# A two-layer hybrid diffusion step on one core: projections in pieces between the steps of the scans, PSUM divided six banks to two

## The chip, the core and the metric

One core of a Trainium2 chip runs the whole program. Its engines run on their own and meet at semaphores: TensorE (PE, matmuls, with PEld for its weight loads), VectorE (DVE), ScalarE (ACT), GpSimd (POOL) and SyncE (SP, which issues most DMAs). Each takes its instructions strictly in the order of the program. SBUF holds the data; PSUM, in which matmuls leave their results, has eight banks of 512 fp32 columns. The metric is the time of the device in microseconds (us); lower is better.

## The reference, cut to what matters

Two layers, each over 128 context tokens and 512 latent tokens (640 in all, five tiles of 128), width 1024, all fp32:

```python
def layer(x, p, l, mod, ctx):
    x = half_ffn(x, 0, 0)                    # x + 0.5*gate * rmsnorm(swiglu(modulate(rmsnorm(x))))
    h = modulate(rmsnorm(x, g[2]), mod[:, 3], mod[:, 4])
    y, new = token_mixing(h, p, l, ctx)
    x = x + mod[:, 5][:, None] * rmsnorm(y, g[3])
    return half_ffn(x, 1, 2), new

def token_mixing(h, p, l, ctx):
    u = h @ p['w_in'][l]                     # 15 blocks of 256 columns, and 48 columns of gates
    ...  # A gated linear attention, C mLSTM, D retention: scans forward and backward over chunks, summed
    ...  # B attention: context to context; latent to a window of 16 columns with a bias, and to the cache
    y = concatenate([out_a, out_b, out_c, out_d]) @ p['w_out'][l]
```

## The kernel before

**Layout and precision.** Activations lie with features on the partitions: `xT` is the residual (8 blocks of 128 features by 640 tokens), `h2` the normed input as a high and a low part. Each large product is made of three matmuls (`three_pass`, L460 to L462: high by high, high by low, low by high). The weights are split into the two parts on POOL (`split`, L419 and L421: a copy that rounds to the high part, then a subtraction over the same 2048 columns for the low part), into two buffers `w_split` by turns. SP loads the raw weights in units of up to 1 MB into two slots (L363), each when the unit two before has been split or used.

**Units.** The layer is a list of 132 units. `U_FFN[0]` are the first FFN's (22 up units of 96 matmuls by 320 columns, 16 down units of 66; between the up units lie small units of the modulation, L471). Then come one unit of gates (160 columns), 15 of the input projection (four each for C, A and D, three for B) and four of the output projection (`U_OUT`), and then the second FFN. Unit n uses banks 0 to 3 or 4 to 7 (`half(n)`); PE takes it up when its split is done and the bank half was evacuated (`claim`: `split_done`, `unit_evac`). A unit of the projection is either `features` (result with features on the partitions, 2 x 2 x 8 x 3 = 96 matmuls of 320 columns) or `tokens` (5 x 8 x 3 = 120 matmuls of 256 columns). DVE, in a few cases ACT, evacuates a whole unit with one instruction of 1280 columns.

**The mixing.** PE's order is written out by hand: gates, five units (C's four and A's first), a wait until DVE and ACT have made the gate rows of C, turned copies of these rows (L613), then C's scans forward and backward, one unit, A with one unit ahead of each direction, two units, D, three units of B, the attention of B, the four output units. In a scan (`scan_group`, L622 to L661) PE first multiplies keys and values for the five tiles (L622), which DVE masks; DVE then carries the states along (L1341). After that a step per tile: scores of tile t+1 (L639; for C also L634), DVE's mask or decay (L1296, for C after an exponential on ACT), output of tile t (L654, L661), DVE's copy (L1304 to L1315). Scans use banks 0 to 7, so no unit of the projection runs inside one. After a group's two directions DVE norms the output per head (`head_norm`, L1369 to L1385, with a root from ACT, `head_rstd`), PE turns it (`concat`), ACT copies it to `catP`.

The attention of B runs 20 blocks (five tiles by four heads; the first four have 128 keys, the other 16 have 640): PE turns the probabilities of block b (L613), makes the scores of block b+2 (L460 to L462), multiplies by the values (L824); DVE adds the bias and finds the maximum (L1620 to L1628), ACT takes the exponential, DVE norms (L1637). The bias table is masked once before, at L1607. Then the four units of the output projection run, and the norm of their sum (`norm(3, ...)`, `add_square`, L1160, `sums`, L492) ends the stage.

## Time and profile before

| | us |
|---|---|
| median of 3 runs | 3450.99 |
| lowest, highest | 3434.47, 3455.9 |
| the profiled execution | 3443.74 |
| its span, first to last instruction | 3442.0 |
| PE busy in it | 3089.8 |
| PEld, DVE, POOL, ACT busy | 2914.7, 1176.2, 1143.6, 526.2 |

The page gives for each engine the time in which it had an instruction in work; a PE that is shown busy need not be at its full rate, since matmuls overlap and since its clock is granted at one of two levels (1.0 in the tables is 2.4 GHz, 0.5 is 1.2 GHz; the figure of a stretch is a mean). The two layers run the same program one after the other, so what is read in the first counts twice. In the first layer the mixing lies between 631.0 and 1198.8 us of the span.

### The profile page before, as it was taken

What the parts mean: (1) busy time and instruction counts of PE and PEld (TensorE: products, weight loads), DVE (VectorE), ACT (ScalarE), POOL (GpSimd) and SP (SyncE); (2) the same over time, 40 slices, a digit from 0 to 9 for tenths busy, and PEclk for the clock granted to TensorE, in tenths of its full rate; (3) what the DMA queues carried; (4) which work ended last, traced back from release to release, by engine and by line L of the source; (5) the groups of instructions that cost most, each with busy time, mean ns of one, the idle gap of its engine ahead of it and who ended that gap; (6) DMA issues with size and microseconds to landing.
All of it is one profiled execution on the core that took longest, in us unless ns stands there. A gap on an engine that the chain in (4) does not pass through costs nothing.

```text
span 3442.0 us, 49578 instructions
## 1 busy us (share of the span) xinstructions
PE 3089.8 (90%) x21080; PEld 2914.7 (85%) x21080; DVE 1176.2 (34%) x1613; ACT 526.2 (15%) x866; POOL 1143.6 (33%) x388
## 2 busy tenths in 40 slices
PE   6999998978888889999779999989789888999996
PEld 3999898868877889999749999989688777899996
DVE  3110112363565454133331101133635654531332
ACT  2000001211112321001120000121112132210111
POOL 1344335313021324444314444443131113344442
PEclk9999999979788989999869999999797889999998
DMA  6332332101011111221163333321010101122211
GB/s 248 139 118 91 129 128 87 46 35 41 28 43 50 37 49 66 75 86 58 34 225 122 119 105 124 119 78 51 30 53 16 65 28 49 40 71 79 74 66 56
DMA packets 45630, 271.92 MB, mean 79 GB/s; under 512 B 5120, under 2 KB 10752, under 8 KB 19520
## 3 DMA queue, kind: packets, MB, share of 16 engines
q1 hardware_dynamic: 38736, 259.99, 21.1%
q10 hardware_dynamic: 6768, 10.11, 0.9%
q8 instruction: 96, 1.57, 0.2%
q14 instruction: 30, 0.25, 0.0%
HBM read 265.35 MB, written 4.73 MB: 78 GB/s over the span
## 4 chain that ended last, share of the span: by engine, by line
PE 41%; DVE 5%; ACT 2%; issue 1%; DMA 1%; DVEq 1%; ACTq 0%; PEldq 0%; SPq 0%
PE ps L460 12%; PE ps L462 12%; PE ps L461 12%; PE ps L654 1%; DMA first_raw<-in_w_mod 1%; ACT arena L854 1%; ACT rstd L854 1%; PE ps L622 1%; PE ps L661 1%; PE ps L471 1%; DVE rstd L1205 1%; PE ps L613 0%; PE ps L639 0%; DVE rstd L1160 0%; PE ps L492 0%
## 5 line engine op out<-in xcount | busy, mean ns | idle before, releaser
L460 PE MATMUL ps<-h,wsplit 128*128 128x320 f32 (+1 forms) x3520 | 1104.0, 314 | 57.2 <-DVE rstd L1205 25.6
L461 PE MATMUL ps<-h,wsplit 128*128 128x320 f32 (+1 forms) x3520 | 1093.5, 311 | 0.0
L462 PE MATMUL ps<-h,wsplit 128*128 128x320 f32 (+1 forms) x3520 | 1093.4, 311 | 0.0
L419 POOL TENSOR_SCALAR wsplit<-raw 128x2048 fp32r<-128x2048 f32 (+1 forms) x192 | 333.3, 1736 | 2239.7 <-issue 1032.4
L421 POOL TENSOR_TENSOR wsplit<-raw,wsplit 128x2048 fp32r<-128x2048 f32 (+1 forms) x192 | 810.1, 4219 | 16.0
L460 PEld LDWEIGHTS ps<-h,wsplit 128*128 128x128 f32 (+1 forms) x3520 | 663.9, 189 | 83.5 <-DVE rstd L1205 45.7
L461 PEld LDWEIGHTS ps<-h,wsplit 128*128 128x128 f32 (+1 forms) x3520 | 664.0, 189 | 0.5
L462 PEld LDWEIGHTS ps<-h,wsplit 128*128 128x128 f32 (+1 forms) x3520 | 663.2, 188 | 0.5
L460 PE MATMUL ps<-hidden,wsplit 128*128 128x320 f32 x1408 | 436.1, 310 | 7.7 <-DVE hidden L1208 4.8
L462 PE MATMUL ps<-hidden,wsplit 128*128 128x320 f32 x1408 | 435.1, 309 | 0.0
L461 PE MATMUL ps<-hidden,wsplit 128*128 128x320 f32 x1408 | 435.0, 309 | 0.0
L1205 DVE TENSOR_TENSOR rstd<-rstd,ps 128x640 f32<-128x640 f32 x88 | 72.3, 821 | 655.6 <-ACT rstd L854 655.6
L854 ACT ACTIVATE rstd<-ps 128x640 f32<-128x640 f32 x88 | 62.0, 705 | 1433.0 <-PE ps L462 1433.0
L460 PEld LDWEIGHTS ps<-hidden,wsplit 128*128 128x128 f32 x1408 | 264.3, 188 | 10.6 <-DVE hidden L1208 5.9
L1208 DVE TENSOR_TENSOR hidden<-rstd,hidden 128x640 f32 (+1 forms) x88 | 235.0, 2671 | 90.7 <-ACT hidden L854 90.7
L461 PEld LDWEIGHTS ps<-hidden,wsplit 128*128 128x128 f32 x1408 | 264.3, 188 | 0.0
L462 PEld LDWEIGHTS ps<-hidden,wsplit 128*128 128x128 f32 x1408 | 264.3, 188 | 0.0
L460 PE MATMUL ps<-wsplit,h 128*128 128x256 f32 x720 | 210.6, 293 | 3.9 <-ACT arena L854 2.9
L461 PE MATMUL ps<-wsplit,h 128*128 128x256 f32 x720 | 209.1, 290 | 0.0
L462 PE MATMUL ps<-wsplit,h 128*128 128x256 f32 x720 | 208.8, 290 | 0.0
L854 ACT ACTIVATE arena<-arena 128x640 f32<-128x640 f32 (+3 forms) x102 | 84.2, 831 | 641.1 <-DVE rstd L1160 224.8
L460 PEld LDWEIGHTS ps<-wsplit,h 128*128 128x128 f32 x720 | 144.1, 200 | 7.9 <-ACT arena L854 3.4
(173 smaller groups left out, 2759.5 us busy)
## 6 DMA issues: line engine op xcount, KB each, us to landing
raw<-in_w SPq DMA_DIRECT2D x88, 1024.0 KB, 6.2
raw<-in_w_mod SPq DMA_DIRECT2D x48, 1024.0 KB, 4.8
raw<-in_w SPq DMA_DIRECT2D x64, 704.0 KB, 4.1
raw<-in_w_in SPq DMA_DIRECT2D x30, 1024.0 KB, 4.8
first_raw<-in_w_mod SPq DMA_DIRECT2D x24, 1024.0 KB, 4.9
raw<-in_w_out SPq DMA_DIRECT2D x8, 1024.0 KB, 5.0
arena<-in_rpb ACTq DMA_DIRECT2D x2, 1792.0 KB, 7.2
xT<-in_x ACTq DMA_DIRECT2D x1, 2560.0 KB, 11.2
```

The costliest lines, as they stand in the source:

```text
L419: nc.gpsimd.tensor_scalar(w[:, 0], src, 1.0, 1.0, ALU.mult, ALU.mult).then_inc(pool_hi, 1)
L421: nc.gpsimd.tensor_tensor(w[:, 1], src, w[:, 0].bitcast(FP), ALU.subtract)\
L460: mm(out, w[0], x[0], start=first, stop=False)
L461: mm(out, w[0], x[1], start=False, stop=False)
L462: return mm(out, w[1], x[0], start=False, stop=last)
L471: last = mm(ps[strip, half(n):half(n) + 256], cond[:, k, :], w[:, k, :], start=k < 4, stop=k >= 4)
L622: last = mm(ps[:, c:c + 2 * vw], kt[:, t, f * P:(f + 1) * P], v[:, t, 2 * f * vw:2 * (f + 1) * vw], start=True, stop=True)
L654: last = mm(ps[:, o + h * vw:o + (h + 1) * vw], Asb[t % 2][:, a, f, :], v[:, t, h * vw:(h + 1) * vw], start=h == 0, stop=own, skip_group_c ...
L661: last = mm(ps[:, c:c + 2 * vw], qi[:, f, t * P:(t + 1) * P], s, start=g == G_C and f == 0, stop=True, skip_group_check=True)
L854: return act.activation(out, in_, f, **kw)
L1205: V.tensor_tensor(halves(rstd[:, :]), halves(rstd[:, :]), acc(half(n) + 2 * BANK), ALU.mult)\
L1208: V.tensor_tensor(lo[:, at], rstd[:, :], hi[:, at].bitcast(FP), ALU.subtract)\
```

## The change

It rewrites the mixing stage of each layer.

- **Pieces.** The 15 input units and the first part of the output projection are cut into pieces that each fill less than one bank of 512 columns: `feat` (24 matmuls of 320 columns, four to a unit), `tok` (two token tiles, 48 matmuls of 256 columns, or one tile), `pre` (one matmul of A's decay). Pieces use banks 6 and 7 by turns; everything else of the mixing has banks 0 to 5. `dense(count)` issues the next pieces; the table `FILL` says how many stand before a scan, after its first products, and between scores and output of each of its five steps.
- **Evacuation.** ACT evacuates every piece (`drain`), at places in its own program written to answer PE's; piece p waits for the evacuation of piece p-2. For the first two units of B, ACT writes the high part and DVE (`lows`) the low part.
- **Scan.** In C, scores of tile t now wait until DVE has read the output of tile t-2 (`ot_done`, before: `a_done`), since both lie in one bank. DVE gets work between its steps: A's log decay inside the scan before, D's rotation inside A's second scan, `lows` inside D's.
- **Output projection.** The first six of eight input blocks (A, C, D) in 16 pieces of 18 matmuls (`U_O1`), one in each of the 16 long blocks of the attention; the last two (B) after it as one unit of 96 matmuls (`U_O2`), which DVE adds. The mask of the bias table moves from before the attention to after its second block.
- **Residual.** `xT` (2.5 MB) is written to device memory before the scans and read back before the norm; its place holds A's and D's data in between. A DMA of ACT's queue each way.
- **Gates.** One block of 96 columns instead of two of 96 and 64; the rows of both directions lie on partitions 0 to 7.
- **Split.** POOL's two instructions for each unit become four and four, each over a quarter of the columns, in every stage (the FFNs too).

```diff
+PARTS = 4
...
+FEAT = [("feat", m, a) for m in range(2) for a in range(2)]
+TOK = [("tok", 0, 2), ("tok", 2, 2), ("tok", 4, 1)]
+PRE = [[("pre", 2 * z + f, a) for f in range(2) for a in range(2)] for z in range(2)]
+PIECES = []
+for _u, _parts in ((U_C, FEAT), (U_C + 1, FEAT), (U_C + 2, TOK), (U_C + 3, TOK),
+                   (U_A, TOK), (U_A + 1, FEAT), (None, PRE[0]), (U_A + 2, FEAT), (U_A + 3, TOK),
+                   (U_D, TOK), (None, PRE[1]), (U_D + 1, TOK), (U_D + 2, TOK), (U_D + 3, TOK),
+                   (U_B, FEAT), (U_B + 1, FEAT), (U_B + 2, TOK),
+                   (U_O1, FEAT), (U_O1 + 1, FEAT), (U_O1 + 2, FEAT), (U_O1 + 3, FEAT)):
+    PIECES += [(_u, *_p) for _p in _parts]
+BY_DVE = [p[0] in (U_B, U_B + 1) for p in PIECES]
+AFTER = {p[0]: i + 1 for i, p in enumerate(PIECES) if p[0] is not None}
+AFTER[U_O2] = len(PIECES) + KT
+
+FILL = {(0, 0): (1, 1, 1, 1, 1, 1, 1), (0, 1): (5, 1, 1, 1, 1, 1, 1),
+        (1, 0): (4, 1, 1, 1, 1, 0, 0), (1, 1): (0, 1, 1, 0, 1, 0, 0),
+        (2, 0): (0, 1, 1, 1, 1, 0, 0), (2, 1): (0, 1, 1, 1, 1, 0, 0)}
...
+        spill = nc.dram_tensor("spill", (P, KT, NTOK), FP, kind="Internal").ap()
...
+        BANK_OF = lambda p: (6 + p % 2) * BANK
...
-                        if k >= SLOTS:
+                        if k >= SLOTS and SPLIT[k - SLOTS] in AFTER:
+                            pool.wait_ge(dense_done, AFTER[SPLIT[k - SLOTS]])
+                        elif k >= SLOTS:
                             pool.wait_ge(unit_done, i * du + UD(SPLIT[k - SLOTS]))
                         pool.sem_inc(split_begun, 1)
                         w, src = split_ap(n, words), slot_ap(n, words)
-                        nc.gpsimd.tensor_scalar(w[:, 0], src, 1.0, 1.0, ALU.mult, ALU.mult).then_inc(pool_hi, 1)
-                        pool.wait_ge(pool_hi, i * 2 + (k + 1))
-                        nc.gpsimd.tensor_tensor(w[:, 1], src, w[:, 0].bitcast(FP), ALU.subtract)\
-                            .then_inc(split_done, 1)
+                        step = words // PARTS
+                        for q in range(PARTS):
+                            at = slice(q * step, (q + 1) * step)
+                            nc.gpsimd.tensor_scalar(w[:, 0, at], src[:, at], 1.0, 1.0, ALU.mult, ALU.mult)\
+                                .then_inc(pool_hi, 1)
+                        for q in range(PARTS):
+                            at = slice(q * step, (q + 1) * step)
+                            pool.wait_ge(pool_hi, i * (2 * PARTS) + (k * PARTS + q + 1))
+                            nc.gpsimd.tensor_tensor(w[:, 1, at], src[:, at], w[:, 0, at].bitcast(FP), ALU.subtract)\
+                                .then_inc(split_done, 1)
...
+                    def dense(count):
+
+                        for _ in range(count):
+                            p = next(line)
+                            n, kind, i, j = PIECES[p]
+                            if p >= 2 and BY_DVE[p - 2]:
+                                pe.wait_ge(dense_dve, N_DVE[p - 2])
+                            elif p >= 2:
+                                pe.wait_ge(dense_act, N_ACT[p - 2])
+                            if kind == "pre":
+                                last = mm(ps[:, BANK_OF(p):BANK_OF(p) + HALF], wa2[64:96, i * P:(i + 1) * P],
+                                          GX[64:96, j * HALF:(j + 1) * HALF], start=True, stop=True)
+                                last.then_inc(dense_done, 1)
+                                continue
+                            pe.wait_ge(split_done, SD(n))
+                            nk = 6 if n >= U_O1 else KT
+                            w = split_ap(n, nk * 256).rearrange("p s (k c) -> p s k c", k=nk)
+                            if kind == "feat":
+                                for k in range(nk):
+                                    last = three_pass(ps[:, BANK_OF(p):BANK_OF(p) + HALF],
+                                                      [w[:, v, k, i * P:(i + 1) * P] for v in range(2)],
+                                                      [h2[:, v, k, j * HALF:(j + 1) * HALF] for v in range(2)],
+                                                      k == 0, k == nk - 1)
+                            else:
+                                for t in range(i, i + j):
+                                    c = BANK_OF(p) + (t - i) * GW
+                                    for k in range(KT):
+                                        last = three_pass(ps[:, c:c + GW],
+                                                          [h2[:, v, k, t * P:(t + 1) * P] for v in range(2)],
+                                                          [w[:, v, k, :] for v in range(2)], k == 0, k == KT - 1)
+                            last.then_inc(dense_done, 1)
...
+                        dense(fill[1])
...
+                            if t >= 2 and g == G_C:
+                                pe.wait_ge(ot_done, R(g, z, t - 2))
+                            elif t >= 2:
                                 pe.wait_ge(a_done, R(g, z, t - 2))
...
                         scores(0)
-                        if (g, z) == (G_C, 0):
-                            pe.wait_ge(kt_ready, 2)
                         for t in range(NT):
                             if t + 1 < NT:
                                 scores(t + 1)
+                            dense(fill[2 + t])
                             output(t)
...
+                    dense(11)
...
+                    dense(3)
...
+                    dense(1)
                     pe.wait_ge(ot_done, R(G_C, 1, NT - 1))
-                    features(U_A + 1)
...
+                    dense(2)
                     pe.wait_ge(ot_done, R(G_A, 1, NT - 1))
-                    tokens(U_D + 2)
                     concat(2)
...
+                    dense(3)
                     pe.wait_ge(ot_done, R(G_D, 1, NT - 1))
-                    features(U_B)
                     concat(3)
...
+                        if b == NH:
+                            pe.wait_ge(cat_split, 6)
+                        if b >= NH:
+                            dense(1)
                         na_values(b)
...
-                    def cat_ready(k):
-
-                        if k in (0, CAT_K[3]):
-                            pe.wait_ge(cat_split, KT if k else CAT_K[3])
-
-                    for q in range(4):
-                        features(U_OUT + q, cat_ready if q == 0 else None, out_part if q == 3 else None)
+                    pe.wait_ge(split_done, SD(U_O2))
+                    pe.wait_ge(cat_split, KT)
+                    pe.wait_ge(dense_act, N_ACT[-1])
+                    w = split_ap(U_O2, SLOT_W).rearrange("p s (k c) -> p s k c", k=2)
+                    for m in range(KT):
+                        if m >= 4:
+                            pe.wait_ge(y_sum, m - 3)
+                        for a in range(2):
+                            c = (2 * (m % 4) + a) * BANK
+                            for k in range(2):
+                                last = three_pass(ps[:, c:c + HALF],
+                                                  [w[:, v, k, m * P:(m + 1) * P] for v in range(2)],
+                                                  [h2[:, v, 6 + k, a * HALF:(a + 1) * HALF] for v in range(2)],
+                                                  k == 0, k == 1)
+                        last.then_inc(dense_done, 1)
+                    pe.wait_ge(y_sum, KT)
...
+                    def drain(count):
+
+                        for _ in range(count):
+                            p = next(tail)
+                            n, kind, i, j = PIECES[p]
+                            act.wait_ge(dense_done, p + 1)
...
+                    act.dma_start(spill, xT).then_inc(spilled, 16)
+                    act.dma_start(wa2[64:96, :], I["wa2"][l]).then_inc(wa2_loaded, 16)
...
+                        state_out(G_C, z)
+                        drain(fill[1])
                         for t in range(NT):
                             act.wait_ge(wl_done, z * NT + t + 1)
                             fn(WL[t % 2], WL[t % 2], ACT.Exp).then_inc(w_ready, 1)
-                            if t == 0:
-                                state_out(G_C, z)
+                            if t:
+                                drain(fill[1 + t])
+                        drain(fill[1 + NT])
...
+                        drain(sum(fill[2:]))
+                        if z == 0:
+                            decays(1)
+                            state_in(G_A, 1)
+                    drain(2)
+                    act.drain()
+                    fn(Ga, Ga, ACT.Silu).then_inc(act_gate, 1)
+                    head_rstd(1)
+                    state_in(G_D, 0)
+                    concat(2)
...
+                    act.drain()
+                    fn(Gd, Gd, ACT.Silu).then_inc(act_gate, 1)
+                    drain(1)
                     head_rstd(2)
-                    fn(Gd, Gd, ACT.Silu).then_inc(act_gate, 1)
+                    drain(2)
+                    act.dma_start(rpb, I["rpb"][l]).then_inc(rpb_loaded, 16)
+                    act.wait_ge(spilled, 16)
+                    act.dma_start(xT, spill).then_inc(reloaded, 16)
+                    act.dma_start(O["nak"][l], knew).then_inc(na_out, 16)
+                    act.dma_start(O["nav"][l], Vn[:, 0, :]).then_inc(na_out, 16)
+                    for k in range(4):
+                        cat_upper(k)
                     concat(3)
-
...
+                    def lows(count):
+
+                        for _ in range(count):
+                            p = next(lower)
+                            n, kind, i, j = PIECES[p]
+                            f = 2 * (n - U_B) + i
+                            cols = slice(j * HALF, (j + 1) * HALF)
+                            dve.wait_ge(dense_hi, N_DVE[p])
+                            V.scalar_tensor_tensor(qk2[:, 1, f, cols], ps[:, BANK_OF(p):BANK_OF(p) + HALF],
+                                                   QSCALE if n == U_B else 1.0, qk2[:, 0, f, cols].bitcast(FP),
+                                                   ALU.mult, ALU.subtract).then_inc(dense_dve, 1)
...
+                            if between:
+                                between(t)
...
+                        scan_group(G_A, z, C("block"),
+                                   lambda f, t: small[:, DEC_AT[z] + f * NT + t:DEC_AT[z] + 1 + f * NT + t],
+                                   rotate if z else (lambda t: log_decay(1, t - 1) if t else None))
+                        if z == 0:
...
+                                   lambda t: lows(1) if t else None)
...
+                        if b == 1:
+                            cat_lower(4)
+                            cat_lower(5)
+                            dve.wait_ge(rpb_loaded, 16)
+                            r3 = rpb.rearrange("p (m c) -> p m c", c=HD)
+                            V.tensor_tensor(r3, r3, C("namask").unsqueeze(1).to_broadcast([P, 14 * NH, HD]), ALU.add)
+                            dve.drain()
...
-                    V.tensor_copy(halves(yT[:, KT - 1, :]), acc(b + 2 * BANK)).then_inc(unit_evac, 1)
+                    for m in range(KT):
+                        dve.wait_ge(dense_done, len(PIECES) + m + 1)
+                        V.tensor_tensor(halves(yT[:, m, :]), halves(yT[:, m, :]), acc(2 * (m % 4) * BANK), ALU.add)\
+                            .then_inc(y_sum, 1)
+                        if m >= 2:
+                            add_square(3, m - 2)
                     for k in (KT - 2, KT - 1):
                         add_square(3, k)
```

In the pieces of the diff that are left out, DVE's evacuations of units go away, buffers get new places, and PE's calls of `dense` between the stages follow the list of `PIECES`.

## Rows read from the trace of the kernel before

**Rows 1.** The windows view; its first line names the columns; mixing of layer 1.

```profile
core 0: us, PE busy (x) PEld busy (x) DVE busy (x) ACT busy (x) POOL busy (x), PEclk, DMA share, GB/s
631.00:1198.80 567.80, 494.29 (x3341) 460.67 (x3339) 273.10 (x437) 106.67 (x200) 127.62 (x38) 0.86 0.13 43
707.10:730.00 22.90, 6.91 (x53) 6.39 (x53) 12.52 (x11) 4.65 (x9) 6.84 (x2) 0.55 0.13 47
852.20:880.50 28.30, 22.09 (x126) 19.70 (x126) 12.69 (x29) 2.54 (x4) 7.55 (x2) 0.69 0.14 47
995.00:1012.80 17.80, 14.41 (x117) 12.95 (x117) 12.16 (x24) 1.28 (x1) 0.00 (x0) 0.87 0.06 16
1058.60:1071.00 12.40, 5.99 (x24) 4.01 (x22) 7.59 (x19) 3.75 (x12) 6.37 (x2) 0.60 0.31 106
```

**Rows 2.** Timeline of DVE (start, duration, idle before): evacuations of three following units.

```profile
649.87 1.49 DVE L1258 TENSOR_SCALAR arena<-ps 128x1280 f32<-128x1280 f32 x1 [8.85 <-PE ps L462]
663.95 1.49 DVE L1256 COPY arena<-ps 128x1280 f32<-128x1280 f32 x1 [12.59 <-PE ps L462]
678.35 1.49 DVE L1269 TENSOR_SCALAR arena<-ps 128x1280 f32<-128x1280 f32 x1 [12.91 <-PE ps L462]
```

**Rows 3.** Timeline of PE: the outputs of following steps in C, then in D.

```profile
774.71 1.10 PE L654 MATMUL ps<-arena 128*128 128x65 f32 x8
777.93 1.11 PE L654 MATMUL ps<-arena 128*128 128x65 f32 x8
...
1004.95 1.10 PE L654 MATMUL ps<-arena 128*128 128x64 f32 x8 [0.93 <-DVE arena L1296]
1007.13 1.10 PE L654 MATMUL ps<-arena 128*128 128x64 f32 x8
```

**Rows 4.** Timeline of PE: one long block of the attention, turn to turn.

```profile
1117.79 0.77 PE L613 MATMUL ps<-const,arena 128*128 128x128 f32 x5
...
1120.12 1.09 PE L824 MATMUL ps<-arena 128*64 128x128 f32 x8 [0.39 <-ACT arena L854]
...
1121.35 0.77 PE L613 MATMUL ps<-const,arena 128*128 128x128 f32 x5
```

**Rows 5.** The lines view of POOL by form: busy us, mean ns, idle before.

```profile
L421 POOL TENSOR_TENSOR wsplit<-raw,wsplit 128x2048 fp32r<-128x2048 f32 x126 | 588.1, 4668 | 10.5
L419 POOL TENSOR_SCALAR wsplit<-raw 128x2048 fp32r<-128x2048 f32 x126 | 243.2, 1930 | 1863.6 <-issue 965.0 <-DMA raw<-in_w 552.6 <-PE ps L462 346.0
L421 POOL TENSOR_TENSOR wsplit<-raw,wsplit 128x1408 fp32r<-128x1408 f32 x64 | 215.2, 3362 | 5.4
L419 POOL TENSOR_SCALAR wsplit<-raw 128x1408 fp32r<-128x1408 f32 x64 | 87.6, 1368 | 367.1 <-PE ps L462 227.9 <-DMA raw<-in_w 71.8 <-issue 67.4
```

**Rows 6.** Timeline, first FFN: a unit's split on POOL and its first matmul on PE.

```profile
403.35 1.90 POOL L419 TENSOR_SCALAR wsplit<-raw 128x2048 fp32r<-128x2048 f32 x1 [10.42 <-DMA raw<-in_w]
405.34 4.61 POOL L421 TENSOR_TENSOR wsplit<-raw,wsplit 128x2048 fp32r<-128x2048 f32 x1
...
411.16 0.41 PE L460 MATMUL ps<-h,wsplit 128*128 128x320 f32 x1 [0.68 <-DVE rstd L1205]
```

**Rows 7.** Timeline of DVE: the same addition beside a split of POOL, and without.

```profile
591.55 4.18 DVE L1160 TENSOR_TENSOR rstd<-rstd,arena 128x640 f32<-128x640 f32 x1 [0.86 <-ACT arena L854]
...
1691.38 0.82 DVE L1160 TENSOR_TENSOR rstd<-rstd,arena 128x640 f32<-128x640 f32 x1
```

**Rows 8.** Timelines of DVE and ACT: head norm after A, mask of the bias table.

```profile
929.35 1.49 DVE L1376 TENSOR_TENSOR arena<-arena 128x1280 f32<-128x1280 f32 x1
...
933.06 1.28 ACT L854 ACT_TABLE_LOAD   x1
...
936.20 1.49 DVE L1385 TENSOR_TENSOR arena<-arena 128x1280 f32<-128x1280 f32 x1
...
1035.66 3.89 DVE L1607 TENSOR_TENSOR arena<-arena,const 128x3584 f32<-128x3584 f32 x1 [1.47 <-DMA arena<-in_rpb]
```

**Rows 9.** The page, DMA issues: KB each and us to landing, of the residual's size.

```profile
xT<-in_x ACTq DMA_DIRECT2D x1, 2560.0 KB, 11.2
```

765 lines of the change are left out of this document (378 added, 387 removed).

## The prediction

> **What bounds the kernel now.** I read the page first: PE is busy for 90% of the span, and the chain that ended last runs mostly over its three-pass matmuls, so the kernel is PE's, and only time in which PE waits or runs at the low clock can be won. The windows view shows where that is. The mixing of layer 1 takes 567.8 us, with PE 494.3 busy at a mean clock of 0.86 [rows 1]; outside it PE runs on without a gap but for the norms. Inside it the projection units follow each other at full rate: 14.08 us for a `features` unit, 14.40 for a `tokens` unit [rows 2]. The loss lies between them. PE waits for C's gates (6.9 busy in 22.9 us), a scan that follows such gaps runs at 0.69 of the clock and takes 28.3 us where a like one at 0.87 takes 17.8, and the start of the attention has 6.0 busy in 12.4 [rows 1]. So the low clock costs as much as the waits: step for step D's scan at full clock needs only 2.18 us and C's 3.22 [rows 3].
>
> **The work that PE keeps.** The change takes almost no matmul away, so I price the mixing after as PE's work at full clock plus the waits that I still find when I follow the new orders of PE, ACT and DVE against each other. Work: six `features` units x 14.08 + nine `tokens` units x 14.40 + the output projection, as many matmuls as before, 4 x 14.08 = 270.4 us [rows 2]. C: 5 steps x 3.22 + about 1.8 for the opening products = 17.9 a direction, 35.8 for both. A and D: 5 x 2.18 + 1.8 = 12.7 a direction, 50.8 for four [rows 3]. The long attention blocks: 3.56 us from turn to turn less the 0.39 of waiting = 3.17, x 16 = 50.7, and some 7 for the four short ones [rows 4]. 80 turned tiles at 0.15 (five in 0.77) are 12, and for the decay products and gate columns I put 7. Sum 434 us. Against 567.8 that is 134 us a layer, and it is the most that can be won there.
>
> **The waits that stay,** per layer. (a) C's scores now wait for DVE to have read an output that lies in the same bank; that is two short DVE operations and two hand-overs, which I put at 1.1 us, before eight steps: 9. No piece stands in that place. (b) At the seams of C and A: the `pre` pieces are one matmul on PE but two ACT instructions each, C's last fixing of the output (three operations over 1280 columns, 1.49 each by [rows 8]) outlasts the one piece behind it, A's keys are turned through two banks that ACT must empty, and in A's second scan DVE has five operations of D's rotation in each step while `FILL` has no piece at steps 1 and 3: together 15. (c) From A to D: here a cover goes. Before, PE had a unit of 14.4 us during `head_norm`, which took from 929.35 to 937.69 [rows 8]. Now it has two pieces, 8.6 us, and ACT may take up its part only behind their evacuation, then a table load of 1.28 and a SiLU of about as much, then a second table and the root; DVE's last three operations of 1.49 come after that [rows 8]. I follow it to about 11 us of idle PE, 4 more for turning through ACT, and 5 for scans that restart at the low clock: 20. (d) D: keys and decayed queries are made by DVE only when the first direction is over (two operations over 1280 columns, 3 us), and the unfilled steps 3 and 4 carry `lows`: 13. (e) Before the attention ACT has, in this order, the last evacuation, four DMA issues, four casts of `cat_upper`, the copies of `concat(3)`, two more casts and a table: PE gets its first turn 11 us after its last piece, of which 8 are idle. The mask of the bias, 3.89 us on DVE [rows 8], was hidden behind a unit; now it stands with two `cat_lower` between the second and third block, 5.6 us. The ramp of the clock adds 2.5. Together 16.5. (f) After the last block the last two casts and subtractions: 3.5. Sum 77. Unknown here are the hand-overs between engines; half of it (39) and half as much again (116) bound it.
>
> The gates with one block end with the norm that feeds them, some 3 us earlier; that and the start are in the stretch from 632.3 us on. The mixing then takes 434 + 77 + 1.3 = 512 us instead of 567.8: 55 us less a layer, 110 for both.
>
> **Filled steps** cost PE nothing beyond the piece. In a long block DVE and ACT, which fit into 3.56 us before [rows 4], have less to do than PE (3.17 + 18 matmuls x 0.147 = 5.8). There the 16 pieces are free of waits; the 16 blocks take 92 us, 41 more than their own work, and hold 42 of the 56 us of the output projection.
>
> **The split in quarters** reaches every unit. From the forms of 2048 and 1408 columns POOL's subtraction costs 2.04 ns a column and 0.49 us fixed, the rounding 0.88 ns and 0.13 [rows 5]; three more of each are 3 x 0.62 = 1.9 us for a unit, 8.5 instead of 6.6. A down unit gives PE 66 x 0.147 = 9.7 us, its split would take 4.7 + 1.9 = 6.6: hidden. In the first FFN the weights arrive late behind the modulation's: split done at 409.95, used at 411.16 [rows 6], 1.2 us of slack, about the least of all iterations. With 44 such iterations, a quarter of them short by some 0.4, I put 4 us lost; the bounds are 0 and 44 x 0.7 = 31. On the other side DVE waits for less: an addition of 0.82 us took 4.18 beside a split [rows 7], at the end of the FFN and of the mixing, where PE waits for it. With quarters the wait is at most one piece of 1.5, so 2.5 us at two places in each of two layers: 10 won.
>
> The Trainium skill speaks against more splits beside DVE's scans (GPSIMD Engine Reference, "8. Key points": POOL shares its SBUF interfaces with VectorE and contends with DVE instructions that have two SBUF inputs). The trace agrees: 4.18 against 0.82 us [rows 7]. By it all of `head_norm` and the joins of the scans meet POOL's pieces now; at 0.4 us for each of some ten operations on the path that would be 4 us a layer, 3343 instead of 3335.
>
> **The residual** is hidden, 2.5 MB each way: it leaves while the weights of the next two units are already loaded, and comes back before the attention, over 90 us ahead of the norm that needs it. The bounds are nothing and one transfer on the path, 11.2 us for this size [rows 9] a layer.
>
> **The sum,** against the profiled execution: 3443.7 - 110 + 4 - 10 = 3328. The median of the runs is 7 us above that execution, so I forecast 3335 for a median, 0.966 of before. With the bounds of the waits, 3335 - 2 x 38 = 3259 and 3335 + 2 x 39 = 3413.
>
> **Rivals.** *ACT's order holds PE up.* Each of 75 pieces waits for ACT, which takes evacuations in a written order behind its waits for DVE. In favour: PE, DVE and ACT now meet in each step. Against: ACT is busy 107 of 568 us [rows 1], and the pieces' places match. If each of the 59 pieces of the scans and projections lost 1 us more, that is 118 us, and the time 3453; at half of that, 3394. I give the band 3405 to 3480 a chance of 0.11. *PE without gaps:* the waits of (b) to (e) are mostly hidden, 3190 to 3265. Against it speaks (c), where nothing stands in the place. 0.06. *POOL becomes the bound* and the kernel slower: if a piece costs not 0.31 us fixed on the mean but 1 us, a unit's split takes 6.6 + 6 = 12.6; the first FFN's chain then lacks 6 - 2 = 4 us in 44 iterations (176), and a down unit's split of 10.7 exceeds PE's 9.7 in 64 units (64 or more): 3335 + 230 = 3565. It decides from some 0.7 us fixed per instruction on. The fixed parts read from two forms speak against it [rows 5]. 0.06. Other losses of over 1%, as a transfer or a deadline that I overlook: 0.03. *The change does not do what it says* would be pieces that run before or after the scans, as the orders of the engines make impossible.
>
> **How the numbers follow.** 0.74 for the forecast, within 3265 to 3405: the bounds of the waits, narrowed at neither side by more than 8 us. Above 3405 lie 0.11 + 0.09, below 0.06, so the range holds about 0.75 to 0.8. About 1% (3416 to 3486) is what a measurement of this kernel can tell from no change. Faster: 0.74 + 0.06 + 0.05 of the first rival = 0.85. Same: the other 0.06. Slower: 0.09.
>
> **What would show it.** In the profile after: a mixing of 512 us with a mean clock above 0.93; pieces of 3.5 and 5.8 us between scores and outputs; attention blocks 5.8 us apart; PE idle for about 11 us ahead of `concat(2)` and 8 ahead of the first short block; POOL's subtraction of 512 columns at 1.5 us, of 352 at 1.2; up units of the first FFN still 16.4 us apart. Wrong would be waits of PE for ACT's evacuation inside the scans, for the split in the FFNs, or for the residual ahead of the norm.

## The result, and the profile after

The changed kernel takes 3335.28 us (median of 4 runs, 3333.38 to 3339.29) against 3444.95 us before (median of 4). The ratio is 0.9683, with a 95% interval from 0.9647 to 0.9719. Its profiled execution took 3335.24 us, with a span of 3333.3 us. Nine to eleven runs of the kernel before, taken beside each group of experiments, have medians of 3450 to 3452 us; against these the change wins some 115 us, against its own four runs of before 110.

The predicted time is met to a fraction of a microsecond, but not by its own sum. Two terms of it were wrong by nearly 40 us each, in opposite directions. The profile after does not show that by itself; single parts of the change, run alone, did.

First the mixing of layer 1 in the windows view, from 2 us ahead of the first piece (629.4) to the last matmul of the output. It answers [rows 1].

```profile
core 0: us, PE busy (x) PEld busy (x) DVE busy (x) ACT busy (x) POOL busy (x), PEclk, DMA share, GB/s
627.30:1149.30 522.00, 464.36 (x3320) 430.12 (x3320) 252.29 (x435) 133.73 (x267) 157.98 (x160) 0.92 0.16 56
...
910.00:925.00 15.00, 3.25 (x23) 3.08 (x23) 7.95 (x5) 4.97 (x7) 8.50 (x8) 0.65 0.18 61
925.00:940.00 15.00, 12.97 (x81) 10.79 (x81) 4.48 (x7) 4.71 (x9) 0.00 (x0) 0.78 0.03 10
```

522 us instead of 567.8, 46 less. Only 16 of these are idle time of PE (57.6 instead of 73.5); the other 30 are busy time of PE, which fell from 494.3 to 464.4 for as good as the same matmuls, because the granted clock rose from 0.86 to 0.92: laid over PE's busy time, the clock's records put 126.0 us of it at the low level before and 61.9 after, and half of the difference is 32 us. I had counted 55 us less.

The waits of PE in the whole execution (us in total, times, longest), those that name a step of the prediction:

```profile
PE ps L669 <- DVE arena L1523: 23.5, 2, 11.8
...
PE ps L669 <- DVE arena L1766: 13.4, 4, 3.6
...
PE ps L726 <- DVE arena L1427: 10.0, 6, 3.4
...
PE ps L704 <- DVE arena L1445: 8.2, 8, 1.0
...
PE ps L501 <- POOL wsplit L459: 7.8, 2, 3.9
```

The first is the wait ahead of `concat(2)`, one a layer. The second is the start of the attention, the third for the most part the unfilled steps of A's second scan (4.5 of 5.0 us a layer), the fourth C's scores, which wait for an output to be read. The last seems to be a wait for a split, and is none: that split had ended at 1115 us. PE starts the last output unit at 1133.55, when DVE has just ended the two `cat_lower`, which took 2.65 us beside the next unit's split:

```profile
1130.79 2.65 DVE L1498 TENSOR_TENSOR h<-arena,h 128x640 fp32r<-128x640 f32 x2 [0.80 <-ACT h L925]
```

POOL's forms in the lines view (busy us, mean ns), which answer [rows 5]:

```profile
L459 POOL TENSOR_TENSOR wsplit<-raw,wsplit 128x512 fp32r<-128x512 f32 x480 | 653.3, 1392 | 0.0
L454 POOL TENSOR_SCALAR wsplit<-raw 128x512 fp32r<-128x512 f32 x480 | 294.9, 641 | 1413.9 <-issue 634.6 <-DMA raw<-in_w 520.4 <-PE ps L503 258.9
L459 POOL TENSOR_TENSOR wsplit<-raw,wsplit 128x352 fp32r<-128x352 f32 x256 | 239.4, 966 | 0.0
L454 POOL TENSOR_SCALAR wsplit<-raw 128x352 fp32r<-128x352 f32 x256 | 127.2, 524 | 302.8 <-PE ps L503 180.7 <-DMA raw<-in_w 65.6 <-issue 56.5
```

The addition now takes 0.87 us where it took 4.18 [rows 7]:

```profile
591.48 0.87 DVE L1297 TENSOR_TENSOR rstd<-rstd,arena 128x640 f32<-128x640 f32 x1 [0.86 <-ACT arena L925]
```

For the comparisons below I cut each execution at the last multiplication of each norm (one DVE instruction, the same in every kernel) into three stages a layer: the first feed-forward part, the mixing with its norm, and the second feed-forward part. Where one number stands it is the mean of both layers. The layers can differ: the mixing took 575.9 and 580.2 us in `e1`, 598.2 and 590.4 in `e2`, 604.7 and 593.2 in `e3`, 592.3 and 596.2 in `e11`, but 562.2 and 562.3 after the change.

| kernel | median us | first FFN, layer 1 / 2 | mixing | second FFN |
|---|---|---|---|---|
| before | 3450.5 | 609.6 / 605.8 | 610.7 | 497.1 |
| after | 3335.3 | 606.5 / 602.0 | 562.3 | 494.6 |
| after, whole split (`e1`) | 3379.6 | 610.3 / 605.2 | 578.1 | 497.4 |
| after, halves (`e10`) | 3349.9 | 605.2 / 601.3 | 570.2 | 494.2 |
| after, eighths (`e5`) | 3328.0 | 610.9 / 606.5 | 554.3 | 494.1 |
| before, quarters (`e2`) | 3403.3 | 607.7 / 601.7 | 594.3 | 494.1 |
| after, lumped (`e3`) | 3409.5 | 608.2 / 601.8 | 599.0 | 494.6 |
| lumped, with idle matmuls (`e11`) | 3399.2 | 604.7 / 601.9 | 594.3 | 495.0 |
| after, early gate (`e6`) | 3310.5 | 605.3 / 602.0 | 550.3 | 494.7 |
| combined, mixed split (`e12`) | 3274.8 | 608.2 / 602.7 | 532.9 | 492.6 |

(The median of before in this table is that of the runs beside `e1` to `e4`; beside the other experiments it was 3451 to 3452, beside the changed kernel's own four runs 3445.)

### The profile page after: what moved, and what is told of

Same layout as the page of the kernel before. It is cut to its first block and busy times, and to the rows that moved or that the text cites. A ratio compares the mean times of both kernels' runs of the same rounds, so it can differ in the third digit from the quotient of the medians.

```text
span 3333.3 us, 51220 instructions
## 1 busy us (share of the span) xinstructions
PE 3022.2 (91%) x20984; PEld 2845.8 (85%) x20984; DVE 995.3 (30%) x1609; ACT 585.5 (18%) x1008; POOL 1367.0 (41%) x1556
## 5 line engine op out<-in xcount | busy, mean ns | idle before, releaser
L454 POOL TENSOR_SCALAR wsplit<-raw 128x512 fp32r<-128x512 f32 (+2 forms) x776 | 441.3, 596 | 1924.6 <-issue 899.0
L459 POOL TENSOR_TENSOR wsplit<-raw,wsplit 128x512 fp32r<-128x512 f32 (+2 forms) x776 | 932.3, 1233 | 0.0
L925 ACT ACTIVATE arena<-ps 128x512 f32<-128x512 f32 (+3 forms) x198 | 86.2, 456 | 383.1 <-PE ps L503 297.3
```

The costliest lines, as they stand in the source:

```text
L454: nc.gpsimd.tensor_scalar(w[:, 0, at], src[:, at], 1.0, 1.0, ALU.mult, ALU.mult)\
L459: nc.gpsimd.tensor_tensor(w[:, 1, at], src[:, at], w[:, 0, at].bitcast(FP), ALU.subtract)\
L925: return act.activation(out, in_, f, **kw)
```

## The experiments

### The two parts of the change, each alone

`e1` takes the split in quarters out of the changed kernel, `e2` puts it into the kernel before.

```diff
-PARTS = 4
+PARTS = 1
```

> The changed kernel with the split undone: two POOL instructions for each unit again, all else as changed. My theory: the quarters are worth what the feed-forward stretches won (3.1, 2.5, 3.8 and 2.5 us, 12 in all, because VectorE waits for at most one short piece of POOL), so this kernel takes 3335 + 12 = 3347 us, and up to 3357 if VectorE's instructions inside the scans, which now stand on TensorE's path, also wait for whole splits of 4.6 us. Rival: the quarters only add fixed time to POOL and delay the split in the first feed-forward part (the 4 us that I had booked as a loss): then this kernel is faster, 3325 to 3332. Third: the quarters do nothing, 3333 to 3338.

> The kernel before with only the split in quarters. My theory: the feed-forward stretches win 10 to 12 us as in the changed kernel, and the mixing, where TensorE runs whole units and seldom waits for VectorE, 0 to 4: 3445 - 13 = 3432 us (3427 to 3437). Rival: the quarters cost, since the first feed-forward part has only 1.2 us of slack for the split: 3445 to 3475.

Measured: `e1` 3379.59 us (ratio to before 0.9794, 0.977 to 0.9817), `e2` 3403.28 us (0.9866, 0.9842 to 0.989). So the quarters are worth 44 us in the new kernel and 47 in the old one, and the placing of the pieces, with everything else in the change, 71 us (63 to 79 by the interval of `e1`; 68 if read from `e2` to the changed kernel). My theory (12) and all rivals fall. The feed-forward stages win the 12 us that I expected there (table). The rest, 16 us a layer, is won in the mixing, where I had expected 0 to 5. It is a mean: 14 and 18 us in the two layers of the new kernel, 12 and 20 in those of the old one. In the new kernel it is time in which PE waits (69.7 us idle in layer 1 of `e1`, 57.6 after the change), not the clock, which is 0.92 in both.

The mechanism is that of [rows 7], at many more places than two. These are the same instructions of the gates in `e1` (with POOL's subtraction beside them) and in the changed kernel:

```profile
653.11 5.07 POOL L459 TENSOR_TENSOR wsplit<-raw,wsplit 128x2048 fp32r<-128x2048 f32 x1
...
653.62 4.58 DVE L1593 COPY small<-arena 8x5 f32<-8x5 f32 x1
658.11 0.13 DVE L1594 COPY small<-par 8x1 f32<-8x1 f32 x1
...
658.40 0.16 DVE L1597 COPY small<-arena 8x5 f32<-8x5 f32 x1
```

```profile
646.84 0.58 DVE L1593 COPY small<-arena 8x5 f32<-8x5 f32 x1
647.33 0.13 DVE L1594 COPY small<-par 8x1 f32<-8x1 f32 x1
...
648.07 1.19 DVE L1597 COPY small<-arena 8x5 f32<-8x5 f32 x1
```

With whole splits one copy of five columns stands for 4.58 us until POOL's subtraction ends at 658.18, and the next ones run freely. With quarters more of them are held, but none of these copies takes more than 1.2 us. DVE's busy time in the mixing falls from 270.1 us (`e1`) to 252.3, and in the old kernel from 273.1 [rows 1] to 257.6 (`e2`). The Trainium skill has this rule (SBUF — State Buffer, "SBUF: two separate sides": between a GpSimd instruction and a VectorE instruction that is in a two-port mode or has two SBUF inputs, whichever starts first has the shared ports for its whole instruction, and the other is blocked); these rows agree, the copy ends 0.02 us after the subtraction.

A held instruction can cost more than its length. In the kernel before, such a hold of 3.9 us (5.53 instead of 1.63) lies shortly ahead of the first scan of D (DVE, the held instruction, then copies of the outputs of following steps):

```profile
966.87 5.53 DVE L1577 TENSOR_TENSOR arena<-arena,const 128x1024 f32<-128x1024 f32 x1
...
988.13 0.42 DVE L1313 COPY arena<-ps 128x256 f32<-128x256 f32 x1 [2.16 <-PE ps L661]
...
992.14 0.42 DVE L1313 COPY arena<-ps 128x256 f32<-128x256 f32 x1 [2.16 <-PE ps L661]
```

and the same in `e2`:

```profile
965.60 1.63 DVE L1584 TENSOR_TENSOR arena<-arena,const 128x1024 f32<-128x1024 f32 x1
...
979.97 0.42 DVE L1320 COPY arena<-ps 128x256 f32<-128x256 f32 x1 [0.83 <-PE ps L668]
...
982.15 0.42 DVE L1320 COPY arena<-ps 128x256 f32<-128x256 f32 x1 [0.83 <-PE ps L668]
```

Steps of 4.01 us became steps of 2.18: the same work, at a clock of 0.50 (984 to 993 us) and of 1.00 (977 to 984 us). That the shorter hold is what let the clock stay up is the likely reading; it was not isolated.

### How finely to split

> The changed kernel with the split in halves. Whole splits 3380, quarters 3335, eighths 3328. Theory: the loss is in proportion to the time of POOL's longest instruction (4.67, 1.39 and about 0.8 us): 44 us for 3.3 us is 13.5 us per us; a subtraction of 1024 columns takes about 2.5 us, so 3335 + 1.1 x 13.5 = 3350 (3345 to 3356). Rival: it is the number of VectorE instructions that meet a split at all, which halves nothing: as whole splits, 3370 to 3380.

> The changed kernel with the split in eighths: eight and eight POOL instructions for a unit. The runs so far gave 44 us for quarters against whole splits, because an instruction of VectorE that needs POOL's idle moment waits for one piece (4.18 us with whole splits, 0.87 with quarters). Theory: the wait still scales with the piece, so pieces of half the length win another 5 to 9 us: 3328 (3323 to 3331). Rival 1: what is left of the wait no longer reaches TensorE's path: 3333 to 3337. Rival 2: POOL becomes the bound; in the first feed-forward part a unit's split takes 7.4 us with quarters and ends 1.8 us before it is used; eight more instructions of 0.2 us fixed each just use that up, at 0.4 us each 1.4 us are short in 44 iterations, +60: 3395.

Halves 3349.89 us (ratio 0.9716, 0.9688 to 0.9744), eighths 3327.99 us (0.9648, 0.961 to 0.9686): both as the theory of a loss in proportion to the piece said. The stages show that this is a coincidence of two things. In the mixing each halving wins about the same, 578.1, 570.2, 562.3, 554.3, 8 us a layer each time as a mean of both layers, and not half of the last gain. The first feed-forward part wins 5.1 and 3.9 us (layer 1 and 2) with halves, then loses about 1 with quarters and 4.5 more with eighths. There PE begins to wait for the split; all 17 of these waits lie in the first feed-forward parts, where the changed kernel has none:

```profile
PE ps L501 <- POOL wsplit L459: 14.5, 17, 1.3
```

So rival 2 was right about the mechanism and wrong about the size. POOL's subtraction takes 4.65 us for 2048 columns, 2.55 for 1024, 1.39 for 512 and 0.80 for 256.

### The places inside the steps

```diff
-FILL = {(0, 0): (1, 1, 1, 1, 1, 1, 1), (0, 1): (5, 1, 1, 1, 1, 1, 1),
-        (1, 0): (4, 1, 1, 1, 1, 0, 0), (1, 1): (0, 1, 1, 0, 1, 0, 0),
+FILL = {(0, 0): (7, 0, 0, 0, 0, 0, 0), (0, 1): (11, 0, 0, 0, 0, 0, 0),
+        (1, 0): (8, 0, 0, 0, 0, 0, 0), (1, 1): (3, 0, 0, 0, 0, 0, 0),
```

> The changed kernel with the pieces of the scans of C and of A placed in one lump ahead of each scan instead of inside its steps (D and the attention keep theirs). My theory: the pieces cover the waits of the steps; without them each of the four scans takes the 28 us that the first scan of A took before, instead of its own work of 13 to 18, so some 10 us a scan come back, 40 a layer, less the waits of 9 + 15 us that the filled steps keep: about +25 a layer, 3385 us (3365 to 3410), and the mean clock falls by 0.01. Rival: what the change gives comes from the covered gates (16 us idle before) and the attention alone, and the places inside the steps are worth nothing: 3335 to 3342.

Measured 3409.48 us (0.9872, 0.9846 to 0.9898): 74 us more than the changed kernel, at the upper end of the expected range, and the mean clock fell by 0.02 where I had said 0.01. That is no better than the old kernel with quarters (3403), but it does not make the rest of the placing worthless. From their first product to their last output the four scans of C and A take 122 us in layer 1 of `e3` and 99 in `e2` (115 and 92 in layer 2): they carry the new wait ahead of C's scores, and C's run at 0.61 instead of 0.75. The whole mixing is only 6.5 us longer (2.8 in layer 2). So the covered gates, D and the attention do bring 17 to 20 us a layer against `e2`, and the unfilled scans of C and A lose them again. The windows of the mixing of layer 1, then a stretch inside C's first scan, then C's second scan in layer 1 and in layer 2, here:

```profile
629.00:1193.00 564.00, 495.85 (x3320) 458.33 (x3320) 246.13 (x435) 133.82 (x266) 149.31 (x160) 0.85 0.15 52
730.00:760.00 30.00, 23.02 (x104) 20.48 (x104) 11.85 (x34) 3.15 (x5) 0.00 (x0) 0.50 0.10 35
796.30:833.90 37.60, 28.52 (x155) 25.15 (x154) 24.51 (x50) 6.27 (x9) 7.43 (x8) 0.62 0.09 33
2494.30:2524.50 30.20, 21.12 (x156) 18.48 (x155) 23.66 (x47) 6.08 (x8) 7.43 (x8) 0.89 0.11 40
```

and the same stretch of C in the changed kernel:

```profile
730.00:760.00 30.00, 29.05 (x191) 26.37 (x190) 13.47 (x32) 9.15 (x17) 8.53 (x8) 0.94 0.14 45
```

Of the 42 us more in this mixing, 31.5 are busy time of PE (495.9 instead of 464.4, with 3320 matmuls in both) and 10.5 idle time. The pieces earn their places less by covering waits than by the clock at which the scan's own matmuls run: 0.50, that is the lower of the two levels (1.2 GHz), against 0.94. What the clock alone is worth stands in the last two rows of `e3`: the same scan of the same kernel takes 37.6 us at a mean of 0.62 and 30.2 at 0.89.

That can be tried with work that is of no use:

```diff
                             dense(fill[2 + t])
+                            if g != G_D:
+                                busy(12)
```

`busy(12)` is 12 matmuls of 320 columns from the normed input into a bank whose content was evacuated, so nothing is computed with them.

> The kernel with the pieces of C and A in lumps, plus 12 matmuls that nobody reads in each step of these four scans (40 steps, 480 matmuls). In the lumped kernel a step of C takes 7.1 us with TensorE at 0.50 of its clock and nearly without waits; at full clock its own work is 3.2. Theory: pieces inside the steps are worth so much because they keep the clock up, and idle work does that too: 3.2 + 12 x 0.147 = 5.0, some 5.3 with what is left of waits, so 1.8 us less for each of 20 steps of C, and a step of A stays at 4.0: 3409 - 36 = 3373 (3360 to 3390), a clock near 1.00 in the scans of C. Rival: the pieces help by covering waits and the clock follows something else; then the added work costs 40 x 1.8 to 3.5 us: 3480 to 3550.

Measured 3399.18 us (0.9859, 0.9831 to 0.9887). The kernel does 480 matmuls more than `e3`, and its median is 10 us lower. The times alone don't prove that it is faster: the intervals of the two ratios overlap, and one of `e3`'s four runs took 3400.3. The traces show what happened. A step of C, first in `e3`, then here (PE's timeline):

```profile
742.41 2.08 PE L704 MATMUL ps<-arena,const 128*128 128x128 f32 x8 [1.02 <-DVE arena L1445]
744.42 1.23 PE L709 MATMUL ps<-arena 64*128 64x128 f32 x8
745.58 1.97 PE L726 MATMUL ps<-arena 128*128 128x65 f32 x8
747.34 1.18 PE L733 MATMUL ps<-arena 128*128 128x130 f32 x4
```

```profile
738.07 1.16 PE L713 MATMUL ps<-arena,const 128*128 128x128 f32 x8 [1.02 <-DVE arena L1456]
739.16 0.71 PE L718 MATMUL ps<-arena 64*128 64x128 f32 x8
739.80 2.02 PE L687 MATMUL ps<-h 128*128 128x320 f32 x12
741.66 1.00 PE L735 MATMUL ps<-arena 128*128 128x65 f32 x8
742.50 0.67 PE L742 MATMUL ps<-arena 128*128 128x130 f32 x4
```

Every group of the scan takes little more than half its time, and the step 6.1 us instead of 7.1. I had expected 5.3: I had left out the wait of 1.02 us that stands ahead of such a step with or without the clock. Nor do all steps win: between the first two outputs of a scan 8.0 us pass instead of 5.7. So a scan of C takes 35.5 us instead of 37.5, at a clock of 0.90, and where `e3` had the clock by itself, in C's second scan of layer 2, it takes 35.6 instead of 30.2. The mixing of layer 1 is 12.4 us shorter, 4.9 of them in the four scans; the units between the scans win too, as the lump behind C's first scan, which runs at 0.95 instead of 0.84 and takes 34.1 us instead of 37.1. The mixing of layer 2 is 3.0 us longer. (Another 3 us of the profiled execution lie in layer 1's first feed-forward part, which the edit doesn't touch.) Idle work does keep the clock up, and it pays only where the clock would have been low. The rival (70 us slower or more) is out.

### The low clock behind a wait

`e4` fills the wait of 11.7 us ahead of `concat(2)` with 70 such matmuls, `e8` the four waits at the start of the attention with 81.

```diff
                     dense(2)
+                    hold(70)
                     pe.wait_ge(ot_done, R(G_A, 1, NT - 1))
```

> The changed kernel with 70 matmuls whose results nobody reads, placed in the wait of 11.7 us ahead of the second concatenation, so that TensorE does not rest there. The wait itself stays as long. My theory: after that wait TensorE runs at 0.50 to 0.78 of its clock for some 10 us, which costs 3.4 us; with the rest filled it restarts at full clock, so 3 to 4 us a layer are won, 3328 us (3325 to 3331), and the windows behind 923.7 us show a clock of 1.00. Rival: the low clock there comes from the second scan of A, which already runs at 0.83, and stays: no gain, or 1 to 3 us lost because the 70 matmuls outlast the wait: 3334 to 3341.

> The changed kernel with 81 matmuls whose results nobody reads in the waits at the start of the attention (28 before the third group of turned tiles, 23 before the first block's turn, 20 before the fourth's, 10 behind it). TensorE ran at 0.50 of its clock from 1017 to 1037 us and at 0.82 from 1037 to 1047. Theory: the long blocks are TensorE's, so the time that the clock cost in them stays won: the low clock costs about 5 us from the first long block on, 3 to 5 us a layer, 3327 (3324 to 3330). Rival: given back as with the 70 matmuls before the second concatenation (0.4 us a layer arrived there): 3334 to 3337.

Measured: `e4` 3335.05 us (0.9666, 0.9647 to 0.9686), `e8` 3336.41 us (0.967, 0.9641 to 0.9699). Neither wins anything that can be seen. In `e4` the clock did come back:

```profile
910.00:925.00 15.00, 13.12 (x94) 12.65 (x92) 8.12 (x5) 5.46 (x8) 8.64 (x8) 1.00 0.19 62
925.00:940.00 15.00, 12.52 (x93) 10.84 (x94) 6.33 (x12) 3.97 (x8) 0.00 (x0) 1.00 0.03 10
```

1.00 where the changed kernel has 0.65 and 0.78, and D's first piece began 2.1 us earlier (933.5 instead of 935.6). But 0.9 of that was lost again in D, where the clock fell at the same time (962.3 us) and so at a later place of the work, and the mixing ended only 0.3 us shorter. At the start of the attention, in the changed kernel and in `e8`:

```profile
1013.00:1041.00 28.00, 18.17 (x61) 13.41 (x62) 20.87 (x40) 10.46 (x27) 2.52 (x2) 0.51 0.38 155
```

```profile
1013.00:1041.00 28.00, 24.80 (x126) 21.36 (x127) 19.86 (x39) 10.09 (x26) 1.72 (x2) 0.82 0.34 141
```

The clock rose from 0.51 to 0.82, and the first long blocks came 0.9 us earlier (counted from the end of the first feed-forward part). So the low clock there costs next to nothing. The likely reason is that PE stands behind DVE and ACT there: DVE is busy for 20 of the 28 us, and `e7` below, which changes the order of ACT's and DVE's work, wins what the clock doesn't. Warming one wait in front of work that has waits of its own is worth nothing here; in `e11` it was worth something where all steps of a scan were at the low clock.

### Taking the waits away

`e6` moves ScalarE's SiLU with its table load ahead of the evacuations of A's second scan, and the root of the head norm ahead of the last two evacuations.

```diff
+                            act.drain()
+                            fn(Ga, Ga, ACT.Silu).then_inc(act_gate, 1)
+                            ln_exp()
                         drain(sum(fill[2:]))
...
+                    head_rstd(1)
                     drain(2)
-                    act.drain()
-                    fn(Ga, Ga, ACT.Silu).then_inc(act_gate, 1)
-                    head_rstd(1)
```

> The changed kernel with ScalarE's SiLU of A's gate (and its table load) moved ahead of the evacuations of A's second scan, and the root of the head norm ahead of the last two evacuations. Theory: TensorE's wait of 11.7 us before the second concatenation is ScalarE's written order; it falls to about 6, and the restart is less cold: 5.7 + 1 us a layer, 3322 (3319 to 3326). Rival: as with the 70 matmuls that kept the clock and whose 2 us were given back in D and at the start of the attention, VectorE (keys, decayed queries) and not TensorE sets the pace behind: the wait falls and at most 2 us a layer arrive, 3331 to 3335.

Measured 3310.48 us (0.9592, 0.9563 to 0.9621): 24.8 us won, where I had expected 13 (3319 to 3326). ACT's timeline in the changed kernel says why:

```profile
909.07 0.60 ACT L925 ACTIVATE arena<-ps 128x512 f32<-128x512 f32 x1 [12.96 <-PE ps L503]
911.95 0.38 ACT L925 ACTIVATE arena<-ps 128x256 f32<-128x256 f32 x1 [2.28 <-PE ps L503]
912.40 1.28 ACT L925 ACT_TABLE_LOAD   x1
913.69 1.27 ACT L925 ACTIVATE xT<-xT 128x1280 f32<-128x1280 f32 x1
914.98 1.28 ACT L928 ACT_TABLE_LOAD   x1
916.27 0.60 ACT L925 ACTIVATE small<-small 128x20 f32<-128x20 f32 x2
```

DVE had its sum ready at 906.1 us. ACT sat idle, with the root behind two evacuations that had to wait for PE's pieces: the pieces that were to cover the head norm held it up. After the root DVE's first two operations of 1.49 us took 2.57 and 2.39, held by a split, which is another 2.0 us of the wait. In `e6` the root is taken at 905.02, and the first turn follows the last piece (ending at 910.8) with no wait, at full clock:

```profile
910.63 1.04 PE L669 MATMUL ps<-const,arena 128*128 128x128 f32 x8
```

`e7` reorders the start of the attention: scores of the first two blocks ahead of `concat(3)`, ACT's DMA issues and casts behind or between the short blocks, one table load less.

> The changed kernel with another order at the start of the attention: scores of the first two blocks before the third concatenation, ScalarE's four DMA issues and six casts behind or between the first blocks, one table load less, the casts' subtractions between the short blocks. Theory: the first turn comes some 6 us earlier, but VectorE has 17 us of work before the first long block (four short blocks, six subtractions of 1.4, the mask of 3.9), so the first long block starts 3 to 4 us earlier: 7 us for both layers, 3328 (3324 to 3331). Rival: VectorE's sum is all that counts and only moves: 3333 to 3337; or the reordering makes it slower.

Measured 3323.69 us (0.9632, 0.9603 to 0.9661): 11.6 us won, where 7 were expected. The first turn comes at 1012.5 instead of 1018.9, and the first scores of a long block at 1025.2 instead of 1031.4; 4.2 us a layer of it are left at the end of the mixing.

Then the gains together:

> Early gate, new start of the attention and split in eighths together, and the cast and subtraction of the seventh part of the concatenation moved ahead of the last blocks. Theory: the three gains (24.8, 11.6 and 7.3 us) lie at different places and add, and the last edit takes 1.4 us from each layer's wait of 3.9: 3335 - 24.8 - 11.6 - 7.3 - 2.8 = 3289 (3284 to 3296). Rival: they overlap, since each of them warms the same stretch: 3296 to 3308.

> The combined kernel with quarters in the first feed-forward part (where a unit's split in eighths is late for TensorE: its last norm ends at 611 us with eighths and at 605 to 606 with quarters) and eighths in the mixing and the second feed-forward part. Theory: the 5 us a layer lost there come back and nothing else changes: 3285 - 10 = 3275 us (3272 to 3279). Rival: the delay in the first part is made up by what the eighths gain at its own end, so that both are the same: 3282 to 3288.

`e9` took 3285.00 us (0.9528, 0.9505 to 0.9552) and `e12`, with quarters up to the gates and eighths from there on, 3274.78 us (0.9494, 0.9477 to 0.9512), which beats both kernels: 60 us under the changed one. Both came out as expected (3289 and 3275), so the gains add. The mixing of layer 1 in `e12`, as above:

```profile
625.50:1129.00 503.50, 460.39 (x3336) 425.65 (x3335) 246.49 (x445) 141.32 (x279) 201.04 (x333) 0.95 0.17 58
```

## Why the prediction was right, and where it was not

**The placing: booked at -110 us, worth -71.** `e1` is the change without the quarters, the case that this term describes. Its mixing has this row, and the sum was 434 of work and 77 of waits and low clock:

```profile
631.00:1163.00 532.00, 462.33 (x3320) 428.31 (x3320) 270.05 (x436) 132.89 (x267) 125.97 (x41) 0.92 0.16 55
```

PE is idle for 69.7 us; my waits, without the 7.5 for the clock, were 69.5. As a sum they fit, partly by luck: this kernel has the holds by whole splits in them, which I hadn't counted; with quarters 57.6 us are idle. The busy time is 462.3 instead of 434, 28 us more, of which I had put 7.5 down to the low clock. This is the step that failed: "I price the mixing after as PE's work at full clock". The clock's records bear it out: PE was busy for 56.6 us of this stretch at the low level, which costs half of them, 28.3, and 462.3 - 28.3 = 434.0 is the work as priced. I had seen that the clock costs as much as the waits, and then charged it at two places only, behind `concat(2)` and at the start of the attention. In the changed kernel the low level also stands ahead of and inside A's scans (860 to 870, 884 to 891 and 901 to 904 us) and inside D (962 to 969). It is 20 us a layer too little.

**The split in quarters: booked at -6 us, worth -44.** Two steps failed. "So 2.5 us at two places in each of two layers" took the two places where I had seen a hold for all there were; the four feed-forward parts alone win 12 us, and the mixing 16 us a layer. And the 4 us lost in the first feed-forward part are not there: its up units are 16.43 us apart before and after. The fixed part of a POOL instruction was over-read too: a unit's split takes 7.4 us there, not 8.5 (a subtraction of 512 columns 1.39 and not 1.5 us, of 352 columns 0.97 and not 1.2).

The two errors are +39 and -38 us, which is why 3335 was met: the agreement to the microsecond is luck. The range did not rest on this luck alone: either error by itself would have missed by no more than 39 us, inside the range.

**The waits, one by one.** (a) C's scores: 1.1 us predicted, 1.02 found, eight in all over both layers, so 4 us a layer and not 9. (b) The seams: 15 predicted; 4.5 ahead of `concat(1)`, 3.2 ahead of A's keys and 5.0 inside A's scans make 12.7. (c) `concat(2)`: 11 predicted, 11.74 found, along the chain that I had named (evacuations, table load, SiLU, second table, root, DVE's three operations), 2.0 of it because a split held two of the last three; what I had not seen is that only ACT's written order made the chain start so late (`e6`). (d) D: 13 predicted, 5.5 found. (e) Before the attention 8 us idle: 4.56 + 3.57 found; at the mask, which stood where I said, 3.1 + 1.6 of the 5.6. (f) 3.5 predicted, 3.9 found.

**The rest.** Long blocks 5.93 us apart (5.8 predicted). The residual was hidden: no wait in the list names it. No wait for an evacuation by ACT inside the scans, but the rival "ACT's order holds PE up" was true at two places, (c) and (e), at prices already in the sum (`e6`, `e7`). "POOL becomes the bound" shows its first waits at eighths; its price was added up wrongly (176 + 64 is 240, not 230, and the slack is the 1.2 us of [rows 6], not 2), which changes nothing here. The forecast of a clock above 0.93 in the mixing failed: 0.92. The warning by which each of some ten operations loses 0.4 us to contention had the right mechanism and the wrong sign: smaller pieces took holds away.

## What to carry to other kernels

Where two engines hold each other up, count every instruction that meets the other one (compare the mean with the shortest duration of each form), not only the two that catch the eye; and cut the long instruction before anything else is moved. Work placed between short matmuls is worth more than the waits it covers if it keeps the clock up, so price busy time at the clock that each stretch will have. A piece that covers a wait must not stand, through its evacuation, ahead of the very instruction that ends this wait.

A prediction that comes out to the microsecond says little about its terms; here only running the parts alone did. And look at both layers of a trace before you use their mean: in `e3` the same scan had another clock in each.

## What the hardware did that I had not expected

- 480 matmuls that compute nothing did not make a kernel slower: the mixing became 12.4 us shorter in the layer whose scans had run at 0.6 of the clock, and 3.0 us longer in the other (`e11` against `e3`). 81 others raised the granted clock only to 0.83 in a stretch where PE was busy for 18.4 of 20 us (`e8`, 1027 to 1047 us).
- The same scan of the same kernel ran at a mean clock of 0.62 in layer 1 and of 0.89 in layer 2 (`e3`).
- Each halving of POOL's instructions, from 2048 down to 256 columns, took 8 to 10 us of DVE's busy time out of the mixing of layer 1 (270.1, 261.7, 252.3 and 242.4 us) and 8 us of its length on the mean of both layers, without a sign of levelling off.
- A DVE copy of 5 columns took 4.58 us beside one subtraction of POOL; others of the same shape, behind it, took 0.15 and 0.16.
